# Two-layer language block with an expert stream: the second mixer's steps set further apart, its attention moved beside the recurrence, and output weight blocks loaded over 128 partitions

## The chip, the cores and the metric

The kernel runs on one core of one Trainium2 chip. The metric is the device time of one execution in microseconds. All data is float32. TensorE (PE) makes matrix products and transposes, VectorE (DVE), ScalarE (ACT) and GpSimd (POOL) compute and issue, SyncE (SP) issues the weight loads, and 16 DMA engines move the data. Each engine works through its own instructions in order and waits on semaphores for the others.

## The reference

256 tokens of width 1024 go through a first block of two layers and then through a second block of two. In the first block each layer is a mixer, an output product with a residual and a layer norm, and a sparse feed-forward layer with its own residual and norm:

```python
for i in range(2):
    z = x @ w_in                      # layer 0: mLSTM, layer 1: RG-LRU (below)
    hm = mixer(z[:, :-256]); ha = cross_attention(z[:, -256:], mem, w_kv[i])
    x = layer_norm(ALPHA * x + concat([hm, ha]) @ w_out[i])
    x = layer_norm(ALPHA * x + peer_ffn(x, w_q[i], subkeys[i], u[i], v[i]))
```

The mixer of layer 1 has 8 channel blocks of 96. Its steps are the ones that the change moves:

```python
xr = causal_conv4(z[:, 768:1536]); r = sigmoid(xr @ w_a + b_a); i = sigmoid(xr @ w_x + b_x)
a = exp(-8 * r * softplus(-lam)); u = sqrt(1 - a**2) * (i * xr)
h = scan(h * a + u)                   # over tokens
hm = h * gelu(z[:, :768])
```

Cross attention has 4 heads of 64 over 256 memory rows. The feed-forward layer takes, for each token and each of 8 heads, the 16 best of 16384 experts, and sums gelu(u_e . x) * g * v_e over its 128 experts. The second block (dilated and latent attention, gated) is not touched.

## The kernel before

The function middle() holds the part that the change touches. Its backbone is the expert stream: 2 layers x 2 token tiles of 128 tokens give 4 tiles, each with 128 slots (8 heads x 16 experts), 512 slots in all. For a slot, POOL gathers one row of u and v (8 KB) for each of the 128 tokens into one of nine row buffers (ROWS = 9, line 2712). VectorE makes the dot of the u half with x (dot, line 2225). ScalarE weighs two slots at a time (weigh, lines 2531 to 2541: gelu, gate weight, coefficient on a diagonal). TensorE adds the v half with these diagonals (line 2124). POOL issues the gather of slot n when TensorE has added slot n - 9.

All other work of the middle part stands beside the stream. Each engine runs a loop over slots and, after its work of slot n, runs those pieces of a generator beside() whose due slot, written out in `yield at + k`, is at most n. Here `at = base_of(t)` = 128 (t + 1), so the mixer of layer 1 for token tile t runs beside the stream's tile t + 1, which is the second of the four for t = 0 and the third for t = 1. Within a slot the order is: VectorE the dot, then a piece of the routing of coming slots (route, planned by plan_chunk and the loop behind it), then the mixer piece; TensorE the slot's sums, then the side piece; ScalarE, in even slots alone, the weighing of slots n and n + 1, then the side piece. An engine that waits in a side piece holds back its part of the stream.

The PSUM bank of each product is written out in `homes`, and `order` says in which order the products come, from which the semaphore counts follow. take(name) waits until the product that was in the bank before has been read; ready(name) waits for a product.

The weights pass through a ring of three slots (line 3332, on SP's queue). SP loads the block n when block n - 3 has been used. For each token tile the ring holds, in order, two blocks of w_in for xr and xq, two for the gate, three of w_out (two with 4 x 96 rows, one with 2 x 128 rows) and four of w_q (512 x 1024). SP also loads the gate matrices w_a, w_x (lines 1602, 1603) and rows of norm gains between the blocks, in its own order.

Steps of the mixer, by name and line of the kernel before: inputs, gates, memory_scores, gate_inputs (1936), turn_probabilities (1912), memory_values (1924), turn_mix (1946), out_products (1967), spread_rows (1981) and queries on TensorE; convolve (2317), the softmax maximum, the attention values (2361), the steps of the recurrence (2371 to 2400), the residual (2405) and norm on VectorE; the softmax exponentials, sigmoids (2574), decay, tanh and root (2641, 2642, 2646) and the copies out of PSUM on ScalarE.

Of the kernel before, what the change touches and what calls it, by code (L numbers as in the profile page):

```python
# [112 lines left out]
class Run:  # L113


    def __init__(self, first, count, cols, pieces, ktiles):
        self.first, self.count, self.cols, self.pieces, self.ktiles = first, count, cols, pieces, ktiles
        self.small_loads = None

# [53 lines left out]
def program(nc, a, out, parts=None):  # L173
# [1308 lines left out]
    def middle():  # L1482
# [22 lines left out]
        shared_at = place[0]  # L1505
        prob, prob_t = sb([P, XA_H, T], name="xa_prob"), sb([P, XA_H * NT, P], name="xa_probT")
        th = nc.alloc_sbuf_tensor_at("tanh_y", [RG_B, RG_G, P], F32, offset=shared_at)
        dec = nc.alloc_sbuf_tensor_at("decay", [RG_B, RG_G, P], F32, offset=shared_at + RG_G * P * 4)
# [11 lines left out]
        qT = sb([P, PE_H, 2, NT, P], name="peer_qT")  # L1520
        ids = sb([P, NT * TILE], U32, name="expert_ids")
# [116 lines left out]
        for t in range(NT):  # L1638
# [3 lines left out]
                     ("probT", t, 0): 0, ("probT", t, 1): 1, ("wa", t, 0): 0, ("wa", t, 1): 1, ("value", t): 2,  # L1642
                     ("wx", t, 0): 2, ("wx", t, 1): 0, ("haT", t): 1, ("out", t, 0): 2, ("out", t, 1): 0}
            second = {("turn", 2 * t + 3, 0): 2, ("turn", 2 * t + 3, 1): 0, ("q", t + 1, 0): 4, ("q", t + 1, 1): 1,
                      ("q", t + 1, 2): 3, ("q", t + 1, 3): 2}
            homes.update({name: places[u] for mine in (first, second) for name, u in mine.items()})
            order += spread(2 * t + 2) + list(first)
            order += spread(2 * t + 3, [places[u] for u in (3, 4, 1, 3)]) + list(second)
# [58 lines left out]
        def query_made(k, h):  # L1707
            return base_of(k - 1) + (81, 84, 92, 95)[h // 2]
# [55 lines left out]
        def tensor(pe):  # L1764
# [184 lines left out]
            def out_products(t):  # L1949
                signal, count = read_at_bank[("haT", t)]  # L1950
                pe.wait_ge(signal.sem, count)
# [45 lines left out]
            def beside():  # L1997
# [11 lines left out]
                for t in range(NT):  # L2009
# [36 lines left out]
                    yield at + 66  # L2046
                    spread_rows(2 * t + 3, slice(3, 4))
                    yield at + 70
                    turn_x(2 * t + 3)
                    yield at + 73  # L2050
                    x_read(2 * t + 3)
                    for c in range(2):
                        yield at + 74 + 11 * c
                        yield from paced(queries(t + 1, c), at + 74 + 11 * c, 6)
# [88 lines left out]
        def vector(dve):  # L2143
# [186 lines left out]
            def mixer(t):  # L2330
# [7 lines left out]
                for u, first in ((0, 29), (1, 31)):  # L2338
# [3 lines left out]
                yield at + 33  # L2342
# [5 lines left out]
                for u, first in ((2, 33), (3, 35)):  # L2348
# [6 lines left out]
                yield at + 37  # L2355
# [3 lines left out]
                yield at + 41  # L2359
# [8 lines left out]
                yield at + 43  # L2368

                dve.wait_ge(r_ready.sem, t + 1)  # L2370
                dve.tensor_tensor(r[:, :, :], r[:, :, :], sp[:, :].unsqueeze(2).to_broadcast([RG_B, RG_G, P]), ALU.mult)\
                    .then_inc(y_ready.sem, 1)
                yield at + 45

                dve.wait_ge(decayed.sem, t + 1)
                v(dve.tensor_tensor(r[:, :, :], dec[:, :, :], dec[:, :, :], ALU.mult))
                dve.scalar_tensor_tensor(out=th[:, :, :], in0=r[:, :, :], scalar=1.0, in1=th[:, :, :],
                                         op0=ALU.add, op1=ALU.mult).then_inc(square_ready.sem, 1)
                yield at + 47

                dve.wait_ge(i_ready.sem, t + 1)
                v(dve.tensor_tensor(i_g[:, :, :], i_g[:, :, :], xc[:, :, :], ALU.mult))
                yield at + 48

                dve.wait_ge(rooted.sem, t + 1)
                v(dve.tensor_tensor(i_g[:, :, :], i_g[:, :, :], th[:, :, :], ALU.mult))
                if t:
                    v(dve.tensor_tensor(last_h[:, :], last_h[:, :], dec[:, :, 0], ALU.mult))
                    v(dve.tensor_tensor(i_g[:, :, 0], i_g[:, :, 0], last_h[:, :], ALU.add))
                for g in range(RG_G):  # L2390
                    if g % 4 == 0:
                        yield at + 49 + g // 4
                    v(dve.tensor_tensor_scan(r[:, g, :], dec[:, g, :], i_g[:, g, :], 0.0, ALU.mult, ALU.add))
# [1012 lines left out]
```

## Time and profile before

| | us |
|---|---|
| median of 3 runs | 2535.95 |
| lowest, highest | 2532.78, 2541.17 |
| the profiled execution | 2532.97 |
| its span, first to last instruction | 2531.2 |
| TensorE busy | 2019.9 |
| VectorE busy | 1374.1 |
| ScalarE busy | 709.3 |
| GpSimd busy | 593.3 |

The granted TensorE clock has a mean of 0.891 of full speed over the span. The span falls into a first layer's mixer (to about 227 us), the expert stream (to about 1684 us) and the second block. In the tables below, "DMA share" is the busy share of the 16 DMA engines (sums can pass 1 by a little) and GB/s is what they moved. A row of a timeline has its start, its duration, the engine, the line, the operation, its output and inputs, and in brackets how long the engine was idle before it and for whom it waited.

### The profile page before, as it was taken

How to read it: one execution, taken by the hardware profiler on the slowest of the kernel's cores; microseconds unless marked ns; L12 is line 12 of the kernel's file. 1: busy time of each engine (PE TensorE's matmuls, PEld its weight loads, DVE VectorE, ACT ScalarE, POOL GpSimd, SP SyncE). 2: the span in 40 equal slices, each digit the busy share in tenths (PEclk: the TensorE clock that was granted, in tenths of full speed). 3: DMA queues.
4: the chain of work that ended last, by engine and by line, in shares of the span. 5: the costliest groups of instructions: out<-in, count | busy, mean ns of one | idle time of the engine just before them, and what ended most of it. 6: DMA issues, size and time to landing. Idle time of an engine off the chain costs nothing. (4 is left out here: it accounts for less than half of the span.)

```text
span 2531.2 us, 27949 instructions
## 1 busy us (share of the span) xinstructions
PE 2019.9 (80%) x10229; PEld 1055.6 (42%) x10229; DVE 1374.1 (54%) x3393; ACT 709.3 (28%) x2047; POOL 593.3 (23%) x529
## 2 busy tenths in 40 slices
PE   8998787556858866877866665669998999999998
PEld 5665344111532421442421111116875544886543
DVE  5556856768756468757568875452424422013433
ACT  1132322333343232352322433220014310014230
POOL 0002433444323444433434454420000000000000
PEclk9999899777978977887887778789999999999999
DMA  7636999999989999998999999984742242540431
GB/s 242 224 135 234 398 409 413 420 421 422 390 305 382 419 419 420 420 364 339 417 412 421 421 421 421 421 337 169 274 132 95 76 166 93 176 160 19 156 111 56
DMA packets 186820, 742.34 MB, mean 293 GB/s; under 512 B 26342, under 2 KB 45822, under 8 KB 121144
## 3 DMA queue, kind: packets, MB, share of 16 engines
q0 software_dynamic: 73728, 536.90, 52.0%
q1 hardware_dynamic: 99972, 199.72, 22.2%
q10 hardware_dynamic: 12984, 3.94, 0.7%
q8 instruction: 81, 1.33, 0.2%
q14 instruction: 55, 0.45, 0.0%
HBM read 739.39 MB, written 1.12 MB: 293 GB/s over the span
## 5 line engine op out<-in xcount | busy, mean ns | idle before, releaser
L2124 PE MATMUL psum<-expert_rows,coefs_on_diagonal 64*64 64x512 f32 x4096 | 673.5, 767 | 439.1 <-ACT coefs_on_diagonal L2541 434.5
L2712 POOL DMA_INDIRECT expert_rows<-in_peer_uv,expert_ids x512 | 588.8, 1150 | 1075.1 <-PE psum L2124 810.7
L2225 DVE SCALAR_TENSOR_TENSOR expert_rows<-expert_rows,x 128x1024 f32<-128x1024 f32 x512 | 626.5, 1225 | 375.3 <-DMA expert_rows<-in_peer_uv,expert_ids 359.8
L2124 PEld LDWEIGHTS psum<-expert_rows,coefs_on_diagonal 64*64 64x64 f32 x4096 | 145.9, 157 | 815.2 <-ACT coefs_on_diagonal L2541 610.4
L320 PE MATMUL psum<-xT,ring 128*128 128x256 f32 (+2 forms) x1472 | 322.8, 381 | 1.2 <-DMA ring<-in_mlstm_w_in 1.2
L2531 ACT ACTIVATE gelu_dots<-dots 128x2 f32<-128x2 f32 x256 | 52.1, 203 | 921.1 <-DVE expert_rows L2225 920.9
L320 PEld LDWEIGHTS psum<-xT,ring 128*128 128x128 f32 (+2 forms) x1472 | 268.8, 183 | 57.9 <-issue 10.2
L2541 ACT ACTIVATE coefs_on_diagonal<-ident,coefs 128x128 f32<-128x128 f32 x512 | 177.4, 393 | 8.3
L1800 PEld LDWEIGHTS psum<-xT,ring 128*128 128x128 f32 (+1 forms) x1088 | 130.5, 184 | 81.1 <-issue 81.1
L1800 PE MATMUL psum<-xT,ring 128*128 128x128 f32 (+1 forms) x1088 | 150.3, 289 | 0.0
L2534 ACT ACTIVATE coefs<-gelu_dots,gate_weights 128x1 f32<-128x1 f32 x512 | 123.0, 287 | 8.4
L3157 PE MATMUL psum<-ring,xT 128*128 128x512 f32 x256 | 123.5, 616 | 0.0
L2800 PE MATMUL psum<-ring,xT 128*128 128x512 f32 x192 | 86.2, 610 | 7.8 <-DVE x L2278 4.1
L1827 PEld LDWEIGHTS psum<-xT,ring 128*128 128x128 f32 x512 | 62.7, 197 | 36.8 <-issue 35.8
L1827 PE MATMUL psum<-xT,ring 128*128 128x128 f32 x512 | 71.2, 290 | 0.8 <-ACT xT L2550 0.8
L3157 PEld LDWEIGHTS psum<-ring,xT 128*128 128x128 f32 x256 | 47.5, 195 | 45.0 <-issue 43.1
L3270 ACT ACTIVATE prob<-prob,small 128x256 f32<-128x256 f32 (+3 forms) x96 | 53.2, 557 | 40.1 <-DVE small L3237 39.9
L3280 ACT COPY probT<-psum 128x256 f32<-128x256 f32 (+3 forms) x96 | 37.1, 428 | 95.5 <-PE psum L3191 95.3
L2800 PEld LDWEIGHTS psum<-ring,xT 128*128 128x128 f32 x192 | 37.3, 196 | 55.3 <-issue 51.2
L3034 PE MATMUL psum<-ring,mergedT 128*128 128x512 f32 x128 | 55.6, 594 | 2.8 <-DVEq L3307 2.8
L320 PE MATMUL psum<-ring,ymT 128*128 128x512 f32 x128 | 55.3, 592 | 0.0
L3233 DVE CUSTOM_DVE_ANT_0 prob<-psum,causal 128x256 f32<-128x256 f32 (+1 forms) x64 | 22.9, 358 | 53.6 <-PE psum L3173 52.5
(428 smaller groups left out, 2021.0 us busy)
## 6 DMA issues: line engine op xcount, KB each, us to landing
ring<-in_w_in SPq DMA_DIRECT2D x64, 1024.0 KB
ring<-in_peer_w_q SPq DMA_DIRECT2D x24, 1024.0 KB
first_modulation_weights<-in_w_ada SPq DMA_DIRECT2D x12, 1024.0 KB, 7.4
ring<-in_mlstm_w_in SPq DMA_DIRECT2D x16, 768.0 KB
ring<-in_w_ada SPq DMA_DIRECT2D x12, 1024.0 KB
expert_rows<-in_peer_uv,expert_ids POOLq DMA_INDIRECT x512
ring<-in_rglru_w_in SPq DMA_DIRECT2D x8, 1024.0 KB
ring<-in_w_out_b SPq DMA_DIRECT2D x8, 1024.0 KB
```

The source lines that it names most:

```text
L320: last = pe.matmul(o, l, r, start=first, stop=end)
L1800: ins = pe.matmul(outs[name][0:wide, c * P:(c + 1) * P], w[:, kt, col:col + wide], xT[:, i * run.ktiles + kt, t * P:(t + 1) * P], start=i ...
L1827: last = pe.matmul(out[:, b * P:(b + 1) * P], w[:, kt, b * P:(b + 1) * P], xT[:, kt, t * P:(t + 1) * P], start=kt == 0, stop=kt == KD - 1)
L2124: last = pe.matmul(psum[64 * half:64 * half + 64, 2 * t + m, :], diag[tokens, n % DIAGS, tokens], rows[tokens, at_, D + half * 512:D + (ha ...
L2225: dve.scalar_tensor_tensor(out=rows[:, at_, 0:D], in0=rows[:, at_, 0:D], scalar=1.0, in1=x[:, n // TILE % NT, :], op0=ALU.mult, op1=ALU.mu ...
L2534: ins = act.activation(coef[:, at_ + q:at_ + q + 1], gel[:, at_ + q:at_ + q + 1], ACT.Copy, scale=gw[:, g_at:g_at + 1])
L2541: ins = act.activation(diag[:, (s + q) % DIAGS, :], ident[:, :], ACT.Copy, scale=coef[:, at_ + q:at_ + q + 1])
L2712: pool_.indirect_dma_start(out=rows[:, n % ROWS, :], out_offset=None, in_=table, in_offset=bass.IndirectOffsetOnAxis(ap=ids[:, at_:at_ + 1 ...
L2800: last = pe.matmul(o, l, r, start=first, stop=end)
L3034: last = pe.matmul(o, l, r, start=first, stop=end)
L3157: ins = pe.matmul(o, l, r, start=first, stop=end)
L3270: ins = act.activation(flat, flat, ACT.Exp, bias=columns(0, step)[:, i:i + 1], accum_out=columns(1, step)[:, i:i + 1])
```

## The change

It has two parts. In the first, the due slots of the mixer's steps are moved. The convolution starts two slots later. The w_a products go from slot 40 to 39 and their sigmoids from 42 to 40; VectorE's first step on them stays in 43. Decays stay in slot 44 on ScalarE and are read in 47 instead of 45; the w_x sigmoids stay in 46 and are read in 49 instead of 47; the root comes in 48 and is read in 51 instead of 48. The attention's transposes go from 36 to 48, its values from 40 to 51, and VectorE reads them in 55 instead of 41. The output products are issued from slot 55 to 65 instead of 52 to 62, in three portions, the last one behind the wait for the turned attention output; VectorE adds them in 67 and 68 instead of 62 and 63. The norm after them, its gain rows, the turn of x and the w_q products come four to nine slots later. Bank homes and their order follow. So that the softmax's probabilities can stay until slot 48, the decays and the tanh no longer share their memory; they lie in parts of the query buffer qT that are free then.

In the second, the two w_out blocks of 4 x 96 rows are loaded with 128 partitions: each partition group k takes 128 rows from row 96 k on, so that 32 rows are loaded twice. The products still read 96 partitions.

```diff
+        dec, th = ([qT[0:RG_B, :, s, t, :] for t in range(NT)] for s in range(2))
...
+        def on_all_partitions(run, first):
+
+            run.overlapped = [(bass.AP(a["w_out"].tensor, (D + (first + k) * RG_B) * D, [[D, P], [RG_B * D, 2], [1, D]]), k)
+                              for k in (0, 2)]
+            return run
...
-            rout.append([by_rows(a["w_out"][1], 0, RG_B, 4, 0, D), by_rows(a["w_out"][1], 4 * RG_B, RG_B, 4, 0, D),
-                         by_rows(a["w_out"][1], RG_W, P, 2, 0, D)])
+            rout.append([on_all_partitions(by_rows(a["w_out"][1], i * RG_B, RG_B, 4, 0, D), i) for i in (0, 4)] + [
+                by_rows(a["w_out"][1], RG_W, P, 2, 0, D)])
...
-            return base_of(k - 1) + (81, 84, 92, 95)[h // 2]
+            return base_of(k - 1) + (85, 88, 96, 99)[h // 2]
...
 (tensor, beside)
-                    yield from paced(islice(block, 32), at + 31, 6)
-                    yield at + 36
-                    turn_probabilities(t)
-                    yield at + 37
-                    yield from paced(islice(block, 16), at + 37, 6)
-                    yield at + 40
+                    yield from paced(islice(block, 48), at + 31, 6)
+                    yield at + 39
                     gate_inputs("wa", wa, t, 0)
                     gate_inputs("wa", wa, t, 1)
-                    memory_values(t)
-                    yield at + 41
-                    yield from paced(block, at + 41, 6)
-                    yield at + 44
+                    yield at + 40
+                    yield from paced(block, at + 40, 6)
+                    yield at + 43
                     gate_inputs("wx", wx, t, 0)
                     gate_inputs("wx", wx, t, 1)
-                    yield at + 46
+                    yield at + 48
+                    turn_probabilities(t)
+                    yield at + 51
+                    memory_values(t)
+                    yield at + 55
+                    block = out_products(t)
+                    yield from paced(islice(block, 6), at + 55, 2)
+                    yield at + 58
                     turn_mix(t)
-                    yield at + 52
-                    yield from paced(out_products(t), at + 52, 2)
-                    yield at + 62
+                    yield from paced(islice(block, 10), at + 58, 2)
+                    signal, count = read_at_bank[("haT", t)]
+                    pe.wait_ge(signal.sem, count)
+                    yield at + 63
+                    yield from paced(block, at + 63, 2)
+                    yield at + 65
                     spread_rows(2 * t + 3, slice(0, 3))
...
 (vector, mixer: values after the recurrence instead of before it)
-                yield at + 45
+                yield at + 47
                 dve.wait_ge(decayed.sem, t + 1)
-                v(dve.tensor_tensor(r[:, :, :], dec[:, :, :], dec[:, :, :], ALU.mult))
+                v(dve.tensor_tensor(r[:, :, :], dec[t][:, :, :], dec[t][:, :, :], ALU.mult))
+                yield at + 48
...
-                yield at + 47
+                yield at + 49
                 dve.wait_ge(i_ready.sem, t + 1)
...
-                yield at + 48
+                yield at + 51
                 dve.wait_ge(rooted.sem, t + 1)
...
+                yield at + 55
                 out = ready(("value", t))
...
-                    yield at + 62 + half
+                    yield at + 67 + half
...
 (sync)
+                    for src, k0 in run.overlapped or ():
+                        sp.dma_start(view[:, k0:k0 + 2, :], src).then_inc(landed[slot].sem, 16)
+                    for w, row0, rows, k, k0, p0, col0 in () if run.overlapped else run.pieces:
```

## Rows read from the trace of the kernel before

**Rows 1.** The page, 40 slices of 63.3 us: GB/s of the DMA engines

```profile
GB/s 242 224 135 234 398 409 413 420 421 422 390 305 382 419 419 420 420 364 339 417 412 421 421 421 421 421 337 169 274 132 95 76 166 93 176 160 19 156 111 56
```

**Rows 2.** Windows of the stream's second, third and fourth tile of 128 slots

```profile
core 0: us, PE busy (x) PEld busy (x) DVE busy (x) ACT busy (x) POOL busy (x), PEclk, DMA share, GB/s
587.80:983.80 396.00, 287.42 (x1738) 128.32 (x1738) 257.19 (x597) 134.64 (x408) 148.82 (x128) 0.81 0.98 391
983.80:1366.60 382.80, 284.82 (x1742) 126.32 (x1742) 258.66 (x602) 136.29 (x409) 144.31 (x128) 0.83 0.99 396
1366.60:1683.80 317.20, 193.29 (x1079) 51.39 (x1078) 205.35 (x434) 108.87 (x357) 144.36 (x122) 0.81 1.00 417
```

**Rows 3.** Windows: w_out blocks loading (tile 0, tile 1), and w_q blocks loading

```profile
681.00:696.00 15.00, 11.23 (x94) 6.86 (x87) 11.63 (x30) 8.02 (x25) 4.18 (x5) 1.00 1.02 302
1081.00:1096.00 15.00, 12.16 (x88) 6.96 (x80) 11.96 (x31) 8.60 (x26) 4.83 (x4) 0.89 1.02 335
790.00:820.00 30.00, 22.89 (x102) 6.04 (x104) 17.77 (x36) 11.59 (x30) 10.58 (x10) 0.83 1.02 418
```

**Rows 4.** DMA of 675 to 725 us, then of 1070 to 1120 us

```profile
DMA packets 2757, 17.18 MB, mean 344 GB/s; under 512 B 279, under 2 KB 279, under 8 KB 1047
...
DMA packets 2829, 17.71 MB, mean 354 GB/s; under 512 B 284, under 2 KB 284, under 8 KB 1056
```

**Rows 5.** Windows in the recurrence of tile 0, of tile 1, and the emptiest 10 us

```profile
730.00:790.00 60.00, 41.08 (x165) 13.14 (x166) 42.27 (x88) 24.95 (x64) 15.12 (x15) 0.69 0.81 294
1130.00:1180.00 50.00, 34.57 (x138) 9.43 (x142) 38.19 (x87) 19.02 (x55) 13.20 (x14) 0.76 0.84 312
750.00:760.00 10.00, 3.69 (x16) 0.80 (x16) 9.52 (x22) 2.65 (x8) 2.43 (x2) 0.58 0.41 139
```

**Rows 6.** Waits of VectorE, 695 to 830 us; below the dots, one of 1095 to 1200

```profile
DVE x L2405 <- PE psum L1967: 13.0, 2, 12.8
DVE xa_out L2361 <- PE psum L1924: 7.5, 1, 7.5
DVE r L2371 <- ACT rg_e L2580: 4.7, 1, 4.7
DVE i L2382 <- ACT rg_e L2580: 4.4, 1, 4.4
DVE r L2376 <- ACT tanh_y L2642: 4.3, 1, 4.3
DVE ln_sd L2246 <- ACT ln_sd L2517: 3.1, 1, 3.1
...
DVE x L2405 <- PE psum L1967: 11.5, 1, 11.5
```

**Rows 7.** Timeline of ScalarE and VectorE around slot 43 of tile 0

```profile
721.06 0.20 ACT L2531 ACTIVATE gelu_dots<-dots 128x2 f32<-128x2 f32 x1 [10.18 <-DVE expert_rows L2225]
...
725.99 0.19 ACT L2580 COPY rg_e<-rg_e 1x1 f32<-1x1 f32 x1
...
726.28 1.22 DVE L2371 TENSOR_TENSOR r<-r,sp 96x1024 f32<-96x1024 f32 x1 [4.66 <-ACT rg_e L2580]
```

**Rows 8.** Timeline: gather and dot of the first slot, then of slot 440

```profile
226.83 1.09 POOL L2712 DMA_INDIRECT expert_rows<-in_peer_uv,expert_ids  x1 [220.53 <-DVE expert_ids L2205]
...
236.94 1.22 DVE L2225 SCALAR_TENSOR_TENSOR expert_rows<-expert_rows,x 128x1024 f32<-128x1024 f32 x1
...
1490.65 1.61 POOL L2712 DMA_INDIRECT expert_rows<-in_peer_uv,expert_ids  x1 [0.30 <-issue]
...
1507.81 1.23 DVE L2225 SCALAR_TENSOR_TENSOR expert_rows<-expert_rows,x 128x1024 f32<-128x1024 f32 x1
```

**Rows 9.** Window of slots 44 to 59 beside the mixer of tile 0

```profile
727.40:778.20 50.80, 29.28 (x117) 9.60 (x118) 40.77 (x87) 22.80 (x58) 12.78 (x12) 0.63 0.78 283
```

**Rows 10.** Timeline of TensorE beside the output products of tile 1

```profile
1157.25 1.99 PE L2124 MATMUL psum<-expert_rows,coefs_on_diagonal 64*64 64x512 f32 x8 [1.67 <-ACT coefs_on_diagonal L2541]
...
1173.79 1.09 PE L2124 MATMUL psum<-expert_rows,coefs_on_diagonal 64*64 64x512 f32 x8
1174.81 1.98 PE L1967 MATMUL psum<-ring,xr_conv 96*128 96x512 f32 x4
```

More of the change, by code:

```diff
@@ L1641, in middle @@
                      ("score", t, 0): 0, ("score", t, 1): 2, ("gate", t, 0): 3, ("gate", t, 1): 4,
[L1642 to L1645, printed above, removed]
+                     ("wa", t, 0): 0, ("wa", t, 1): 2, ("wx", t, 0): 1, ("wx", t, 1): 0,
+                     ("probT", t, 0): 2, ("probT", t, 1): 1, ("value", t): 0, ("out", t, 0): 1, ("out", t, 1): 3,
+                     ("haT", t): 2}
+            second = {("turn", 2 * t + 3, 0): 3, ("turn", 2 * t + 3, 1): 1, ("q", t + 1, 0): 0, ("q", t + 1, 1): 2,
+                      ("q", t + 1, 2): 4, ("q", t + 1, 3): 3}
             homes.update({name: places[u] for mine in (first, second) for name, u in mine.items()})
             order += spread(2 * t + 2) + list(first)
-            order += spread(2 * t + 3, [places[u] for u in (3, 4, 1, 3)]) + list(second)
+            order += spread(2 * t + 3, [places[u] for u in (4, 0, 2, 4)]) + list(second)
         last_tile = [("cols",)] + [("hT", half) for half in range(2)] + [("flip", h, part) for h in range(DA_H) for part in range(2)]
@@ L2051, in beside @@
                     x_read(2 * t + 3)
                     for c in range(2):
-                        yield at + 74 + 11 * c
-                        yield from paced(queries(t + 1, c), at + 74 + 11 * c, 6)
+                        yield at + 78 + 11 * c
+                        yield from paced(queries(t + 1, c), at + 78 + 11 * c, 6)
                 yield 3 * TILE + 2
@@ L2337, in mixer @@
                     v(dve.tensor_copy(xr[:, :, 0:CONV - 1], past[:, :, :]))
-                for u, first in ((0, 29), (1, 31)):
+                for u, first in ((0, 31), (1, 33)):
                     yield at + first
@@ L2347, in mixer @@
                 dve.tensor_scalar(negmax[:, :], rowmax[:, :], -XA_D ** -0.5, None, ALU.mult).then_inc(biased.sem, 1)
-                for u, first in ((2, 33), (3, 35)):
+                for u, first in ((2, 35), (3, 37)):
                     yield at + first
@@ L2354, in mixer @@
                     dve.tensor_copy(xr[:, 0, 0:1], xr[:, 0, 0:1]).then_inc(past_kept.sem, 1)
-                yield at + 37
+                yield at + 41
                 dve.wait_ge(exped.sem, x0 + t + 1)
                 v(dve.reciprocal(rowsum[:, :], rowsum[:, :]))
-                yield at + 41
+                yield at + 43
+                dve.wait_ge(r_ready.sem, t + 1)
+                dve.tensor_tensor(r[:, :, :], r[:, :, :], sp[:, :].unsqueeze(2).to_broadcast([RG_B, RG_G, P]), ALU.mult)\
+                    .then_inc(y_ready.sem, 1)
+                yield at + 47
+                dve.wait_ge(decayed.sem, t + 1)
+                v(dve.tensor_tensor(r[:, :, :], dec[t][:, :, :], dec[t][:, :, :], ALU.mult))
+                yield at + 48
+                dve.scalar_tensor_tensor(out=th[t][:, :, :], in0=r[:, :, :], scalar=1.0, in1=th[t][:, :, :],
+                                         op0=ALU.add, op1=ALU.mult).then_inc(square_ready.sem, 1)
+                yield at + 49
+                dve.wait_ge(i_ready.sem, t + 1)
+                v(dve.tensor_tensor(i_g[:, :, :], i_g[:, :, :], xc[:, :, :], ALU.mult))
+                yield at + 51
+                dve.wait_ge(rooted.sem, t + 1)
+                v(dve.tensor_tensor(i_g[:, :, :], i_g[:, :, :], th[t][:, :, :], ALU.mult))
+                if t:
+                    v(dve.tensor_tensor(last_h[:, :], last_h[:, :], dec[t][:, :, 0], ALU.mult))
+                    v(dve.tensor_tensor(i_g[:, :, 0], i_g[:, :, 0], last_h[:, :], ALU.add))
+                for g in range(RG_G):
+                    if g % 4 == 0:
+                        yield at + 52 + g // 4
+                    v(dve.tensor_tensor_scan(r[:, g, :], dec[t][:, g, :], i_g[:, g, :], 0.0, ALU.mult, ALU.add))
+                if t == 0:
+                    v(dve.tensor_copy(last_h[:, :], r[:, :, P - 1]))
+                yield at + 54
+                for u in range(2):
+                    signal, count = read_at_bank[("gate", t, u)]
+                    dve.wait_ge(signal.sem, count)
+                dve.tensor_tensor(xc[:, :, :], r[:, :, :], gate[:, :, :], ALU.mult).then_inc(recurred.sem, 1)
+                yield at + 55
                 out = ready(("value", t))
@@ L2409, in mixer @@
                     norm_stats(t, half)
-                yield at + 64
-                yield from norm(2 * t + 3, t, at + 62)
+                yield at + 69
+                yield from norm(2 * t + 3, t, at + 68)
             def beside():
@@ L3329, in body @@
                         sp.wait_ge(half_done[1].sem, n - (RING - 1))
-                    for w, row0, rows, k, k0, p0, col0 in run.pieces:
+                    for src, k0 in run.overlapped or ():
+                        sp.dma_start(view[:, k0:k0 + 2, :], src).then_inc(landed[slot].sem, 16)
+                    for w, row0, rows, k, k0, p0, col0 in () if run.overlapped else run.pieces:
                         src = w[row0:row0 + rows * k, :].rearrange("(k p) c -> p k c", p=rows)
```

81 lines of the change are left out of this document (26 added, 55 removed).

## The prediction

> **What bounds the kernel now.** I read the 40 slices of the page first. In the expert stream the DMA engines are full and move 420 to 422 GB/s, and two places inside it fall short, slices 12 and 13 (305, 382) and 18 and 19 (364, 339) [rows 1]; these hold the two mixers. Then I took the stream by its tiles of 128 slots [rows 2]. Without a mixer a tile takes 317.2 us, 2.48 us a slot, at 417 GB/s. With the mixer of token tile 0 it takes 396.0 us, with that of token tile 1 382.8 us. Most of that excess is bytes: 391 GB/s over 396.0 us is 154.8 MB, which at 420 GB/s would need 368.7 us. So about 27 us in the first and (151.6 MB, 360.9 us) 22 us in the second are time in which the DMA engines moved less than they can. Only that can be won, and nothing after the third tile changes. The chain of waits on the page shows the last fragments of the output layer alone and says nothing here.
>
> Windows of 10 us sort the lost time into two kinds.
>
> First, while the four blocks of w_out with 96 partitions load, the engines are busy (share 1.02) and slow: 302 GB/s, in token tile 1 335 GB/s, against 418 GB/s while w_q is loaded over 128 partitions beside the same stream [rows 3]. The 50 us around the two blocks move 17.18 MB and 17.71 MB [rows 4]; at 418 GB/s these need 41.1 and 42.4 us. Lost: 8.9 + 7.6 = 16.5 us.
>
> Second, in the recurrence the engines run dry: 294 GB/s over 60 us and 312 GB/s over 50 us, at worst a share of 0.41 [rows 5]. 17.6 MB and 15.6 MB need 42.2 and 37.3 us at 418. Lost: 17.8 + 12.7 = 30.5 us. The rest of the shortfall is in small loads, and I leave it.
>
> **Why they run dry.** VectorE waits in its mixer steps, and the dots of the stream stand behind it in order. Its waits are 7.5 us for the attention values, 4.7, 4.3 and 4.4 us for three results of ScalarE, and 13.0 us for the output products; the second tile repeats them within 1.5 us [rows 6]. One hop is plain in the timeline [rows 7]. ScalarE takes its mixer step of slot 42 only behind the weighing of the pair 42, 43, so after dot 43. VectorE asks for the result in slot 43, right after that dot. Weighing, table load, sigmoids and a copy run from 721.06 to 726.18 us, 5.1 us, and VectorE stands for 4.7 of them. The ring of nine row buffers covers only part of such stops: in the quiet tile a gather is issued 17.1 us before its dot, the first gather of all, with empty queues, needs 10.1 us [rows 8], so some 7 us are slack. VectorE's waits up to the recurrence add to 20.9 us.
>
> **Part 1: steps three slots apart.** It removes no instruction of the engines. In place of a one-slot distance VectorE now asks three slots after ScalarE's step (40 to 43, 44 to 47, 46 to 49, 48 to 51). Between ScalarE's start on the pair and the question there lie two more dots: 2 x 2.48 = 5.0 us against the 5.1 us of the hop. I take 0 to 1 us of wait per hop. The first one may keep 2 to 3 us, since TensorE's products w_a come in slot 39 behind its own queue. The attention values leave the hop altogether: softmax is done at 36, the turns come at 48, values at 51, VectorE reads at 55; 7.5 us become 0. What stands behind VectorE's new waits is as before, the dots; ScalarE's queue carries the same steps, and its new cover is the idle time that it has (busy 22.8 us of 50.8) [rows 9].
>
> VectorE's own work remains: 40.8 us in the 16 slots of the recurrence, against 16 x 2.48 = 39.7 us of rows [rows 9]. It is spread over 13 slots instead of 9, and the 7 us of slack carry it.
>
> The output products start at slot 55 instead of 52 and end at 65, VectorE reads at 67 instead of 62: two slots, 5 us, of distance where there was none. TensorE is the slow one there: 1.09 us for a slot's rows and 1.98 us for two products, 2.93 us from slot to slot [rows 10]. Ten such slots put it 10 x (2.93 - 2.48) = 4.5 us further behind. So of the 13.0 us of wait I expect 3 to 9 us to stay. It costs DMA time only beyond the slack, and from slot 59 on the first w_q block (2.1 MB, 5 us) fills the engines.
>
> Of the steps moved later: the norm waits (root 70, VectorE 73) are three slots apart too and lose their 3.1 us. The w_q products come four slots later, and the routing of the next tile with them: by the planner's arithmetic its first chunk is routed in slot 240 instead of 236, and the gather that needs it is issued after slot 247. SP's load of norm rows ahead of the last w_q block now waits for the step at 75 instead of 66, but that block's ring slot is free only at about 83. The bias tiles start five slots later, with a tile to spare. I cost these at nothing; if routing came after slot 247, each slot of it would cost 2.48 us. That decays and roots lie in the query buffer, rows 512 elements apart, is priced by no row: bound it by 0 and by a tenth of the twelve 1.1 to 1.2 us operations on them, 1.4 us a tile; I take 0.
>
> Residual: the dry time that stays is between 0 and, if the out wait and half the hops empty the ring again, 10 us a tile. I take 5 and 4 us (the first has the gate matrices' short rows too). Part 1 wins 30.5 - 9 = 21.5 us.
>
> **Part 2: the wide blocks.** Each of the four blocks becomes 512 rows of 4 KB instead of 384, 0.52 MB more, 2.1 MB in all: 5.0 us at 418 GB/s. The shape is then that of the w_q load, 128 partitions by two rows of 4 KB to a DMA, and I give it that row's rate, 418 GB/s. It wins 16.5 - 5.0 = 11.5 us. Bounds: 16.5 us less 5.0 at best; at worst the blocks stay at 302 GB/s. Then a block with its share of the stream (1 to 2) is 6.3 MB, 20.9 us, of which the stream alone would need 10.0: 10.9 us of excess against 15.5 - 7.5 = 8.0 now, so 2.9 us more per block, a loss of 11.5 us.
>
> The Trainium skill, page "SBUF — State Buffer", section on the DMA port swizzle, says that bandwidth depends on how many of 16 ports the partitions reach, and partitions 0 to 95 reach all 16. By that rule the narrow block is not slow for its width, and the wide one only adds bytes, which is what rival C works out from rows. The table in the same section of the Trainium skill puts two thirds of 96 partitions on the even ports, and 302 of 418 GB/s [rows 3] is nearer to that. The Trainium skill's section on the bandwidth-pool intuition, same page, gives HBM about 358 GB/s a core; by it the full engines lose little and only some 5 us could be won, but the trace holds 417 GB/s for 317 us [rows 2], so this gets no chance.
>
> **Sum.** Profiled execution 2533 us (span 2531.2 and 1.8 around it): 2533 - 21.5 - 11.5 = 2500 us. The median before, 2536, is 3 us higher within a spread of 8; I predict the sum's own 2500. The two gains add, as both are counted in bytes not moved in windows that do not overlap.
>
> **Rivals.**
> A, the forecast: 2500 us, own range 2492 to 2509. Chance 0.55.
> B, the out products become the bound: ring slack is spent by slot 55 and TensorE's 2.93 us a slot passes straight to the gathers. For it: the lag of 4.5 us and the wait of 13.0 us. Against: w_q fills the engines. 10 us a tile stay dry: 2511 us. Chance 0.15.
> C, the width is not what slows the block: 2533 - 21.5 + 11.5 = 2523 us. For it: no row shows a 96-partition load at full rate beside the stream, so another trait of these blocks could be the slow one. Against: the 128-partition load of the same row length has 418 [rows 3]. Chance 0.10.
> D, all of it comes back: 2533 - 30.5 - 11.5 = 2491 us. Chance 0.10.
> E, no change: C, and the waits only move to other steps (ScalarE's part won 10 us): 2534 us. Chance 0.05.
> F, slower: TensorE runs its out products at the 1.2 GHz level. The granted clock is 0.63 in the recurrence [rows 9], and at that level a slot's rows take 1.99 us [rows 10]. With products at twice 1.98 a slot is 5.95 us, ten are 59.5 us against 24.8, less 12 us of slack and w_q: 23 us a tile, 2546 us. It decides from about 8 of the 10 slots at the low level. Against: within the same stretch the row of 1173.79 has it at the full level [rows 10]. Chance 0.05.
>
> 0.3% of 2533 us, 7.6 us, is what a measurement tells from no change. Faster by more: A to D, 0.90; within: 0.05; slower: 0.05. The range 2489 to 2520 leaves out C, E and F, 0.20.
>
> **What would show it.** The third tile stays at 317 us. The tile of mixer 0 falls to about 378 us, that of mixer 1 to about 368. DMA while w_out loads is near 418 GB/s at the same share: if 300, part 2 is wrong. The three waits of VectorE for ScalarE are under 1 us each and that for the values is gone: if 4 us stand there still, part 1 is wrong. The out wait is 3 to 9 us. No 10 us in the recurrence has a DMA share under 0.8. The prediction falls if VectorE waits for expert ids' routing, or the out products show the low clock.

## The result, and the profile after

The changed kernel takes 2505.1 us (median of 4 runs, 2503.8 to 2507.9), the kernel before 2538.6 us in the same comparison (2532.8 to 2543.4). The ratio is 0.9871, 95% interval 0.985 to 0.9892: 33.5 us faster by the medians. The two profiled executions stand 29.2 us apart (2532.97 and 2503.82 us, spans 2531.2 and 2502.0 us). The forecast was 2500 us, range 2489 to 2520.

The tiles of the stream after the change, windows as in [rows 2] (length, busy time and count of each engine, granted clock, DMA share, GB/s):

```profile
587.00:967.00 380.00, 283.89 (x1730) 125.61 (x1730) 253.01 (x581) 138.40 (x410) 148.95 (x128) 0.82 1.02 414
967.00:1336.40 369.40, 278.00 (x1738) 124.31 (x1738) 259.39 (x601) 137.44 (x410) 147.76 (x128) 0.84 1.01 411
1336.40:1653.60 317.20, 196.43 (x1083) 52.77 (x1083) 209.56 (x449) 109.65 (x359) 143.03 (x121) 0.79 1.00 415
```

The tile with the mixer of token tile 0 fell from 396.0 to 380.0 us and the next from 382.8 to 369.4 us. The third window was cut to the length of the one before, so its 317.2 us say nothing; from the first to the last dot the quiet tile takes 320.3 us instead of 319.4. All of the gain is in the two tiles that were forecast to give it. The DMA engines now move 414 and 411 GB/s there instead of 391 and 396.

While the w_out blocks load, the same two windows as in [rows 3], then the 50 us around the blocks of token tile 0 as in [rows 4]:

```profile
681.00:696.00 15.00, 12.81 (x90) 7.75 (x87) 12.95 (x34) 11.26 (x30) 5.01 (x5) 0.89 1.02 417
1081.00:1096.00 15.00, 13.45 (x112) 8.59 (x109) 7.10 (x13) 11.52 (x28) 6.35 (x6) 1.00 1.02 417
...
DMA packets 3497, 20.85 MB, mean 417 GB/s; under 512 B 318, under 2 KB 318, under 8 KB 1592
```

The share is the same 1.02 as before, the rate 417 instead of 302 and 335 GB/s, and 50 us carry 20.85 MB instead of 17.18. The same engines, as busy, move a fifth more.

VectorE's waits, two stretches that answer to [rows 6], token tile 0 and then 1 (us in total, times, longest):

```profile
DVE expert_rows L2234 <- DMA expert_rows<-in_peer_uv,expert_ids: 55.4, 35, 2.7
DVE x L2415 <- PE psum L1971: 2.2, 2, 1.9
...
DVE expert_rows L2234 <- DMA expert_rows<-in_peer_uv,expert_ids: 30.9, 17, 3.2
DVE expert_rows L2234 <- issue: 2.4, 1, 2.4
DVE x L2415 <- PE psum L1971: 2.1, 1, 2.1
DVE r L2371 <- ACT rg_e L2590: 0.5, 1, 0.5
```

The three waits for ScalarE (but for 0.5 us in token tile 1), the one for the attention values and the one for the norm's root are gone, that for the output products is 2 us. What VectorE waits for now is rows, as it should in a stream that the DMA engines bound. The same hop as in [rows 7], timeline of both engines:

```profile
702.94 0.20 ACT L2541 ACTIVATE gelu_dots<-dots 128x2 f32<-128x2 f32 x1 [6.08 <-DVE expert_rows L2234]
...
707.88 0.19 ACT L2590 COPY rg_e<-rg_e 1x1 f32<-1x1 f32 x1
...
709.36 1.23 DVE L2234 SCALAR_TENSOR_TENSOR expert_rows<-expert_rows,x 128x1024 f32<-128x1024 f32 x1 [1.69 <-DMA expert_rows<-in_peer_uv,expert_ids]
...
711.23 1.22 DVE L2371 TENSOR_TENSOR r<-r,sp 96x1024 f32<-96x1024 f32 x1
```

ScalarE needs the same 5.1 us (702.94 to 708.07). VectorE asks at 711.23, 3.2 us after the result is there, and does not wait for it; it has spent the hop on two dots and on waits for rows.

Slots 44 to 56 and then 56 to 68 of token tile 0, then the same of token tile 1, and the emptiest 10 us, windows:

```profile
712.40:750.10 37.70, 23.64 (x144) 9.54 (x136) 33.91 (x77) 22.76 (x52) 14.65 (x12) 0.72 1.01 415
750.10:782.40 32.30, 31.93 (x128) 9.75 (x129) 19.31 (x37) 12.22 (x39) 11.03 (x11) 0.90 1.04 371
...
1091.20:1130.70 39.50, 22.38 (x144) 9.48 (x144) 31.97 (x77) 27.30 (x61) 15.46 (x12) 0.76 1.00 406
1130.70:1162.10 31.40, 31.26 (x128) 9.52 (x129) 24.52 (x53) 8.62 (x32) 13.43 (x11) 0.93 0.92 360
...
1130.00:1140.00 10.00, 9.16 (x36) 2.77 (x40) 9.62 (x27) 3.16 (x13) 4.16 (x3) 0.73 0.79 287
```

The recurrence is no longer dry. What is still lost lies behind it: 32.3 us at 371 GB/s and 31.4 us at 360 GB/s are, against 418, 3.6 and 4.4 us (length x (1 - rate / 418)); with 0.3 and 1.1 us of slots 44 to 56 that makes 9.4 us.

### The profile page after: what moved, and what is told of

The parts are those of the page before. It is cut to its first block and busy times, and to the rows that moved or that the text cites. A ratio compares the mean times of both kernels' runs of the same rounds, so it can differ in the third digit from the quotient of the medians.

```text
span 2502.0 us, 27950 instructions
## 1 busy us (share of the span) xinstructions
PE 2011.0 (80%) x10229; PEld 1049.1 (42%) x10229; DVE 1375.0 (55%) x3393; ACT 715.0 (29%) x2051; POOL 604.8 (24%) x529
## 5 line engine op out<-in xcount | busy, mean ns | idle before, releaser
L2722 POOL DMA_INDIRECT expert_rows<-in_peer_uv,expert_ids x512 | 600.2, 1172 | 1034.5 <-PE psum L2133 771.9
```

The costliest lines, as they stand in the source:

```text
L2722: pool_.indirect_dma_start(out=rows[:, n % ROWS, :], out_offset=None, in_=table, in_offset=bass.IndirectOffsetOnAxis(ap=ids[:, at_:at_ + 1 ...
```

## The experiments

Every run was timed beside the kernel before on its own chip. The last column is the time from the first to the last dot of the stream. It leaves out the stretches before and behind the stream, which no experiment changes, but it is read from one execution of each kernel.

| kernel | median us | ratio to before, 95% interval | stream us |
|---|---|---|---|
| before | 2537 to 2539 | | 1449.0 |
| changed | 2505.1 | 0.9871, 0.985 to 0.9892 | 1420.2 |
| e1, steps only | 2514.9 | 0.9907, 0.9884 to 0.993 | 1430.9 |
| e2, wide blocks only | 2522.2 | 0.9932, 0.991 to 0.9954 | 1440.0 |
| e3, three hops of one slot | 2512.7 | 0.9894, 0.987 to 0.9919 | 1426.5 |
| e4, values read in 52 | 2502.4 | 0.9852, 0.983 to 0.9875 | 1420.5 |
| e5, 112 partitions | 2518.9 | 0.9918, 0.99 to 0.9936 | 1435.4 |
| e6, 64 and 32 partitions | 2522.6 | 0.9935, 0.9917 to 0.9952 | 1437.6 |
| e7, output products paced | 2501.5 | 0.9854, 0.9836 to 0.9872 | 1418.3 |
| e8, matrices loaded once | 2497.0 | 0.9836, 0.9815 to 0.9856 | 1415.5 |
| e9, e7 and e8 together | 2497.6 | 0.9841, 0.9821 to 0.9861 | 1413.5 |
| e10, one hop of one slot | 2502.6 | 0.9859, 0.9835 to 0.9883 | 1419.7 |
| e11, attention back in front | 2504.5 | 0.9869, 0.9848 to 0.989 | 1420.6 |
| e12, sums read in 65 | 2502.5 | 0.9855, 0.9838 to 0.9872 | 1420.6 |

The medians of kernels whose streams agree within 1 us (changed, e4, e10, e11, e12) lie between 2502.4 and 2505.1, so a difference of 3 us between medians means nothing here. The first and the last tile of the stream, in which nothing differs between these experiments, take 349.5 to 351.5 us and 319.1 to 320.4 us, so a difference of 1 to 2 us in the last column means little too.

**The two parts alone.** e1 is the changed kernel with the narrow blocks:

```diff
-            rout.append([on_all_partitions(by_rows(a["w_out"][1], i * RG_B, RG_B, 4, 0, D), i) for i in (0, 4)] + [
-                by_rows(a["w_out"][1], RG_W, P, 2, 0, D)])
+            rout.append([by_rows(a["w_out"][1], 0, RG_B, 4, 0, D), by_rows(a["w_out"][1], 4 * RG_B, RG_B, 4, 0, D),
+                         by_rows(a["w_out"][1], RG_W, P, 2, 0, D)])
```

> The changed kernel with the two w_out blocks loaded over 96 partitions again. Theory (the narrow blocks slow every packet beside them): 302 to 335 GB/s at a DMA share of 1.02 while they load, 3 us more per block, 11.5 us in all: about 2516 us (2513 to 2520). Rival (the change's gain is the steps alone, the width costs or gives nothing; only 2.1 MB fewer are loaded): 2500 us.

2514.9 us, and the stream is 10.7 us longer. The rate beside the narrow block in e1, window:

```profile
681.00:696.00 15.00, 12.09 (x87) 7.61 (x84) 10.11 (x27) 10.30 (x26) 4.51 (x4) 0.89 1.02 327
```

The rival is out: the width costs what was worked out. e2 is the reverse, the kernel before with the wide blocks (the diff's second part alone).

> The kernel before with the two w_out blocks loaded over 128 partitions, steps as they were. Theory (the two gains add): 2538 less 11.5: about 2527 us, the recurrence runs dry as before (about 17 and 12 us of DMA time lost). Rival (gathers that land earlier before the recurrence only wait there, since VectorE sets the pace): under 4 us gained, 2535 us or more.

2522.2 us, 14.9 us faster by the medians, 9.0 us by the stream. Slots 28 to 44 and 44 to 56 of token tile 0, then of token tile 1, windows of e2:

```profile
662.20:722.70 60.50, 49.15 (x368) 29.95 (x368) 40.52 (x102) 23.91 (x72) 18.45 (x17) 0.94 1.02 417
722.70:766.00 43.30, 21.17 (x105) 7.29 (x102) 33.38 (x75) 20.03 (x48) 11.45 (x10) 0.68 0.78 289
...
1049.20:1109.50 60.30, 48.97 (x376) 30.56 (x376) 38.95 (x89) 26.58 (x74) 19.10 (x18) 0.97 1.02 418
1109.50:1154.80 45.30, 23.82 (x94) 7.88 (x94) 34.95 (x87) 20.82 (x50) 10.49 (x10) 0.62 0.80 304
```

The blocks load at full rate and the recurrence behind them runs dry as before. In token tile 0 the gain arrives: that tile of the stream takes 386.6 us instead of 396.1. In token tile 1 it does not: 383.3 against 382.7 us. There the rival holds: rows that land sooner only wait, since VectorE's stops come next. In one profile each the parts give 18.1 and 9.0 us alone and 28.8 us together: in sum they add to within 1.7 us. By tile they do not. In token tile 1 the wide blocks give nothing alone and 5.9 us once the stops are gone (375.3 us in e1, 369.4 changed); in token tile 0 they give 9.5 us alone and 5.2 us then (385.2 and 380.0).

**Which stops cost.** e3 sets three of VectorE's steps back to one slot behind ScalarE's; e10 sets back the decays alone (the second and third pair of lines):

```diff
-                yield at + 43
+                yield at + 41
                 dve.wait_ge(r_ready.sem, t + 1)
...
-                yield at + 47
+                yield at + 45
                 dve.wait_ge(decayed.sem, t + 1)
...
-                yield at + 48
+                yield at + 46
                 dve.scalar_tensor_tensor(out=th[t][:, :, :], in0=r[:, :, :], scalar=1.0, in1=th[t][:, :, :],
...
-                yield at + 49
+                yield at + 47
                 dve.wait_ge(i_ready.sem, t + 1)
```

> The changed kernel with the three steps of VectorE that read ScalarE's results (sigmoids of w_a, decays, sigmoids of w_x) back to one slot after ScalarE's step: 41, 45 and 47 instead of 43, 47 and 49; the attention stays where it is. Theory: VectorE waits 4.3 to 4.7 us at each again, 13.4 us a token tile. By the two traces 20.9 us of waits before stood for 13.4 us more dry DMA time, 0.64 us each, so 8.6 us a tile: about 2522 us (2515 to 2530). Rival (the ring of nine buffers covers these waits, the attention's move made the gain): 2505 to 2509 us.

2512.7 us, stream 6.3 us longer. Both sides missed: the waits came (below), but they cost under half of what 0.64 us for each us of wait would give. In token tile 1 the same three waits were 7.4, 7.2 and 4.7 us. Waits of VectorE in e3, token tile 0:

```profile
DVE r L2371 <- ACT rg_e L2590: 4.5, 1, 4.5
DVE i L2383 <- ACT rg_e L2590: 4.4, 1, 4.4
DVE r L2376 <- ACT peer_qT L2646: 4.3, 1, 4.3
```

> The changed kernel with one step alone, the decays, read by VectorE one slot after ScalarE's step (45 instead of 47, the square in 46). VectorE waits some 4.3 us in each token tile. If a wait reaches the end in proportion (three of them cost 8 us in all), 2 to 3 us: 2507 to 2508 us and 1 to 2 us of DMA time lost in slots 44 to 56 of a tile. If the nine buffers cover the first 6 to 7 us of waits and no more: 2505 us, under 1 us more lost.

2502.6 us, stream 0.5 us shorter: the wait of 4.3 us (4.8 in token tile 1) costs nothing at the end. Slots 44 to 56 of both token tiles in e10, windows:

```profile
712.60:752.30 39.70, 22.56 (x144) 9.44 (x136) 33.84 (x76) 22.57 (x52) 13.64 (x12) 0.79 1.00 398
...
1090.80:1131.00 40.20, 22.81 (x144) 9.47 (x144) 31.89 (x78) 26.72 (x59) 15.34 (x12) 0.71 0.98 387
```

In these slots 1.9 and 3.0 us of DMA time are lost, 3.5 us more than in the changed kernel, and yet the two tiles of the stream take 378.8 and 370.0 us against 380.0 and 369.4. DMA time lost in a window of a dozen slots is not yet time lost at the end.

e4 moves VectorE's read of the attention values from `at + 55` to `at + 52`, in front of the scans.

> The changed kernel with VectorE reading the attention values in slot 52, one slot after TensorE's step, instead of 55. Theory: VectorE waits some 7 us for the product in each token tile, 4.5 us of it reach the end: about 2514 us (2508 to 2520). Rival (a single wait is covered by the ring): within 2 us of 2505.

2502.4 us, stream the same. But the wait was 1.3 and 1.6 us and not 7, so e4 tells nothing about a wait of 7 us; I had taken the size over from a place where TensorE does other products in the same slot. e11 puts it right. It starts from e2, keeps the attention in its old place and sets the rest apart (ScalarE's sigmoids of w_a stay in slot 42; its decays, sigmoids of w_x and root go to 46, 48 and 50):

```diff
-                yield at + 43
+                yield at + 45
                 dve.wait_ge(r_ready.sem, t + 1)
...
-                yield at + 45
+                yield at + 49
                 dve.wait_ge(decayed.sem, t + 1)
...
-                yield at + 47
+                yield at + 51
                 dve.wait_ge(i_ready.sem, t + 1)
...
-                yield at + 48
+                yield at + 53
                 dve.wait_ge(rooted.sem, t + 1)
...
-                    yield from paced(out_products(t), at + 52, 2)
+                    yield from paced(out_products(t), at + 57, 2)
...
-                    yield at + 62 + half
+                    yield at + 69 + half
```

> The steps set three slots apart (and all behind them later), but the attention where it was before: transposes in 36, values in 40, read by VectorE in 41, in front of the recurrence; blocks of 128 partitions as in the changed kernel. VectorE waits 6 to 9 us for the values again and 0 to 1 us at each of the three hops. If the nine buffers cover one wait of that size and no more: 1 to 3 us over the changed kernel, 2506 to 2508 us. If the attention's move made most of part 1 (three hops alone gave only 8 of its some 20 us): 2513 us or more.

2504.5 us, stream within 0.4 us of the changed kernel. VectorE's waits in e11, token tile 0 and then 1; then windows, slots 44 to 56 of token tile 0, and slots 28 to 44 and 44 to 56 of token tile 1:

```profile
DVE xa_out L2368 <- PE psum L1931: 5.8, 1, 5.8
DVE r L2378 <- ACT rg_e L2588: 0.5, 1, 0.5
...
DVE xa_out L2368 <- PE psum L1931: 8.0, 1, 8.0
...
DVE r L2378 <- ACT rg_e L2588: 2.8, 1, 2.8
```

```profile
712.40:749.00 36.60, 21.72 (x142) 8.21 (x146) 33.45 (x75) 27.79 (x64) 14.70 (x12) 0.82 1.01 420
...
1037.40:1093.30 55.90, 46.56 (x346) 29.20 (x344) 43.32 (x106) 17.64 (x54) 17.67 (x17) 0.94 1.01 412
1093.30:1130.70 37.40, 21.06 (x138) 7.87 (x142) 29.62 (x70) 31.64 (x72) 14.78 (x12) 0.83 1.00 405
```

A stop of 5.8 and one of 8.0 us stand just in front of slot 44 (behind the second one more of 2.8 us, where 0 to 1 was expected), and the engines stay full or nearly so: slots 28 to 68 of token tile 1 lose 7.1 us of DMA time, against 5.6 us in the changed kernel. With the distances in place, the move of the attention gives nothing. Without them it does: e3 has the move and the short distances, and its stream is 13.6 us shorter than that of e2, which has neither (nor the distance of the output products and the norm). So neither the move nor the distances alone made the gain of part 1; each takes stops out of a row. Put in order of waits in a row per token tile: none (changed) 0 us over both tiles; one of 4.3 to 4.8 us (e10) 0; one of 5.8 and one of 8.0 us (e11) 0; three, 13.2 us in token tile 0 and 19.3 in token tile 1 (e3), 6 to 8 us; four, 19.4 and 22.3 us (e2), 17 to 20 us, of which some may belong to e2's waits for the output products, 14.4 and 12.8 us. The nine row buffers cover a stop of about 8 us, and not three that follow each other within a few slots. Which tile pays is not shown: in e3 the tile times rise by 0.8 and 5.7 us, the DMA time lost in slots 44 to 68 by 7.2 and 2.9 us.

e12 has VectorE add the output products in `at + 65 + half` instead of `at + 67 + half`.

> The changed kernel with VectorE adding the output products in 65 and 66 instead of 67 and 68. VectorE waits some 7 us there instead of 2. If that distance matters: 3 to 6 us more over the two token tiles, 2509 us. If VectorE only runs ahead of TensorE there and the w_q blocks keep the DMA engines full behind it: 2505 to 2506 us.

2502.5 us, stream within 0.4 us, with waits of 7.2 and 9.8 us. The two slots of distance gave nothing. Slots 56 to 68 of the two token tiles take 36.1 and 36.4 us instead of 32.3 and 31.4, at 377 and 366 GB/s, so the DMA engines go on at the rate they had. That w_q blocks fill them there is the likely reason; no run takes these away.

**The width.** e5 loads 112 partitions, e6 the 96 rows of each group once, by two DMAs of 64 and of 32 partitions:

```diff
-            run.overlapped = [(bass.AP(a["w_out"].tensor, (D + (first + k) * RG_B) * D, [[D, P], [RG_B * D, 2], [1, D]]), k)
+            run.overlapped = [(bass.AP(a["w_out"].tensor, (D + (first + k) * RG_B) * D, [[D, 112], [RG_B * D, 2], [1, D]]), k)
...
-                        sp.dma_start(view[:, k0:k0 + 2, :], src).then_inc(landed[slot].sem, 16)
+                        sp.dma_start(view[0:112, k0:k0 + 2, :], src).then_inc(landed[slot].sem, 16)
```

> The changed kernel with 112 partitions instead of 128 in the two w_out blocks (448 rows, 1.84 MB a block). Theory 1 (only the full 128, 8 to each of 16 engines as in the stream's own loads, runs at full rate; 6 or 7 to an engine do not): 300 to 340 GB/s as with 96, 2515 to 2519 us. Theory 2 (the halves of the partitions are loaded unevenly, 64 to 48 instead of 64 to 32): about 366 GB/s, 2508 us. Theory 3 (96 is odd, 112 is not): 418 GB/s, 2503 to 2504 us.

```diff
+            run.overlapped = [(bass.AP(a["w_out"].tensor, (D + first * RG_B + p) * D, [[D, n], [RG_B * D, 4], [1, D]]), (p, n))
+                              for p, n in ((0, 64), (64, 32))]
...
+                    for src, (p, n) in run.overlapped or ():
+                        sp.dma_start(view[p:p + n, 0:4, :], src).then_inc(landed[slot].sem, 16)
```

> The changed kernel with each w_out block of 4 x 96 rows (no row twice) loaded by two DMAs, one of partitions 0 to 63 and one of 64 to 95, both over all four row groups, instead of two DMAs over 128 partitions. If the uneven halves are what slows (theory 2), it stays slow, 300 to 340 GB/s: 2513 to 2517 us. If it is the number of partitions that falls to an engine (6), 4 and 2 to an engine may run freely at 418 GB/s and save the 2.1 MB: 2500 us.

The window of 681 to 696 us in e5, then in e6:

```profile
681.00:696.00 15.00, 9.31 (x76) 5.97 (x72) 10.67 (x27) 5.93 (x16) 3.96 (x4) 0.99 1.03 312
```

```profile
681.00:696.00 15.00, 9.85 (x71) 5.25 (x70) 8.92 (x22) 8.27 (x22) 2.81 (x3) 0.91 1.02 292
```

Both are slow at a full share. e5 differs from the changed kernel in the width alone (the narrow blocks too were loaded by two DMAs of two rows per partition each). Its 112 partitions give 312 GB/s, no more than 96, so it is not the share of the halves (366 GB/s expected of that), and it carries more bytes: 2518.9 us, worse than the 2514.9 us of the narrow block. 64 and 32 are the worst, 2522.6 us, over both figures of the expectation; their DMAs have four rows per partition, so here the width is not the only difference. Of the widths tried only 128 is fast, and why is not shown.

**What is left.** e7 spreads the output products, one a slot from 55 and two a slot from 61, and what stands behind them comes two to four slots later.

```diff
-                    yield from paced(islice(block, 6), at + 55, 2)
-                    yield at + 58
+                    yield from paced(islice(block, 6), at + 55, 1)
+                    yield at + 61
                     turn_mix(t)
-                    yield from paced(islice(block, 10), at + 58, 2)
+                    yield from paced(islice(block, 10), at + 61, 2)
```

> The changed kernel with the first 6 output products one to a slot (55 to 60) and the other 14 two to a slot (61 to 67) instead of all 20 two to a slot from 55; VectorE adds them in 70 and 71, and the norm, the turn and the w_q products come three slots later. In the changed kernel nearly all DMA time still lost lies in slots 56 to 68 (3.7 and 4.4 us). Theory (TensorE's 2.93 us a slot passes to the gathers, 10 x 0.45 = 4.5 us a tile): with 2.0 us a slot in six of them under 1 us stays lost, 2505 less 6 to 8: about 2498 us. Rival (VectorE, 96% busy in the 10 us before, empties the ring and TensorE only follows): 2503 to 2506 us.

2501.5 us, between the two figures, and the stream is 1.9 us shorter. But 1.0 and 0.7 us of that are in the stream's first and last tile, which the edit does not touch; the tiles beside the mixers take 379.8 and 369.4 us against 380.0 and 369.4. Slots 56 to 68 of token tile 0 in e7 and then of token tile 1, windows:

```profile
751.60:782.90 31.30, 29.37 (x127) 8.04 (x128) 17.82 (x34) 12.05 (x38) 12.44 (x12) 0.91 1.03 370
...
1132.10:1159.20 27.10, 26.18 (x117) 7.22 (x118) 23.65 (x56) 8.80 (x32) 13.83 (x11) 0.92 0.95 379
```

In token tile 0 370 GB/s against 371 without the edit: taking away TensorE's pace alone changes nothing there. In token tile 1 slots 44 to 68 lose 2.6 instead of 5.5 us, though the tile is no shorter. In token tile 0 the share over 1 at that rate pointed to the load that falls into it, the gate matrices for token tile 1. e8 loads them once; r and i go to the part of qT that the other token tile uses.

```diff
-        wa_at = place[0]
-        r = sb([RG_B, RG_G, P], name="r")
-        wa = nc.alloc_sbuf_tensor_at("w_a", [RG_B, RG_G, RG_B], F32, offset=wa_at)
...
+        wa, wx = sb([RG_B, RG_G, RG_B], name="w_a"), sb([RG_B, RG_G, RG_B], name="w_x")
...
+        rs, i_gs = ([qT[0:RG_B, :, s, 1 - t, :] for t in range(NT)] for s in range(2))
...
-        rq[1][0].small_loads = lambda sp: gate_matrices(sp, 1)
```

> The changed kernel with the gate matrices w_a and w_x loaded once, not again for token tile 1 (they no longer share memory with r and i, which move into the half of the query buffer that the other token tile uses). Theory (the time lost in slots 56 to 68 of token tile 0, 3.7 us, is this load: 0.59 MB in rows of 384 B, 321 GB/s at a DMA share of 1.06; its bytes alone are 1.4 us more): 3 to 4 us faster, 2501 to 2502 us, under 1.5 us lost there. Rival (TensorE's output products are what is lost there, in both token tiles): 1.4 us faster for the bytes, 2503 to 2504 us, 3 us or more still lost.

2497.0 us, stream 4.7 us shorter: more than either figure. The tile with mixer 0 in e8, and its slots 56 to 68, windows:

```profile
587.00:961.90 374.90, 281.80 (x1730) 126.03 (x1730) 252.87 (x581) 138.23 (x410) 146.56 (x128) 0.83 1.01 416
```

```profile
750.50:782.50 32.00, 31.66 (x128) 9.61 (x129) 19.19 (x36) 12.19 (x38) 11.77 (x11) 0.91 0.99 385
```

That tile goes from 380.0 to 374.9 us. 1.4 us of the 5.1 are bytes (0.59 MB at 418 GB/s). The other 3.7 us go with the load too, but only 1.1 of them are found in the slots where it runs (3.6 us lost there before, 2.5 now); that all of them are the slowness of its short rows is not shown, as e8 also moves r and i. 2.5 us stay lost in that window, at 385 GB/s, where under 1.5 were expected. e9 has both edits.

> The paced output products and the gate matrices loaded once, together. If the loss in token tile 0 is the matrices and that in token tile 1 the output products (paced alone lost 3.6 in tile 0 as before and 2.5 instead of 5.5 us in tile 1), the two add: 2505 less 3 less 4, about 2498 us, the fastest so far. If either hides the other: 2501 us.

Slots 56 to 68 of token tile 0 in e9, window:

```profile
752.60:780.70 28.10, 27.75 (x126) 7.55 (x126) 17.78 (x35) 12.09 (x39) 12.21 (x11) 0.94 1.00 409
```

409 GB/s, 0.6 us lost. So that window was held down by both, the matrices and TensorE's pace, and the pace shows only once the matrices are gone (371 to 370 GB/s with them, 385 to 409 without). 2497.6 us, about the 2498 expected, though e8 alone had reached it; stream 2.0 us under e8, 1.1 of them in the two tiles beside the mixers. By the medians e8 and e9 are the same, and e8 is the smaller edit. Both are faster than the changed kernel as far as these runs can tell: the intervals of the ratios overlap (0.9815 to 0.9856 and 0.9821 to 0.9861 against 0.985 to 0.9892), but the streams are 4.7 and 6.7 us shorter, and all ten executions, up to 2500.65 us, lie below the fastest of e10 on the same chip, 2500.84 us, whose stream is that of the changed kernel.

## Why the prediction was right

- **What bounds the kernel.** Right: DMA bytes in the full stretches, and lost DMA time in two places. Counting bytes not moved and pricing them at 418 GB/s gave 33 us; the stream gave 28.8, the profiled executions 29.2 and the medians 33.5. That the medians meet the forecast so closely is partly luck: the median before lies 5.6 us above its profiled execution, the median after 1.3 us. The mechanism was right and the size some 4 us high, 3.4 of them in part 1.
- **The length of a slot.** The 317.2 us of the quiet tile run from its first dot to its 127th, which is 126 slots and not 128: a slot takes 2.51 us, not 2.48. It changes little. Two dots still cover 5.0 us, the output products' lag is 4.2 us instead of 4.5, and VectorE's 40.8 us in 16 slots stand against 40.2.
- **The wide blocks, 11.5 us.** Right: 417 GB/s after, e1 gives 10.7 us by the stream and 9.8 by the medians. Rival C is out.
- **Part 1, 21.5 us.** 18.1 us by the stream in e1, 22.3 by its medians. The residual of 5 and 4 us came out as 3.9 and 5.5 (slots 44 to 68). Its reasons came out in part. In token tile 0 the load of the gate matrices, which the prediction had only named in passing, was the larger part: without it the tile is 5.1 us shorter (e8). The pace of TensorE, which it had made the main one, gave 0.2 us in the two tiles when it alone was taken away (e7) and 1.1 us once the matrices were gone (e9). What holds token tile 1 back behind slot 56 stays open in part. Rival B, 10 us a tile, is out.
- **The hops.** Right in mechanism: 5.1 us of ScalarE behind two dots, waits of 0 to 0.5 us. I had kept 2 to 3 us for the first; 0.5 at most came. The 7 us of slack were read from a single gather, 17.1 us ahead of its dot (the median of slots 400 to 479 is 15.6), but stops of 5.8 and 8.0 us did cost under 1 us (e11).
- **The attention.** The wait of 7.5 us went, as said. That its end is worth something beside the distances was wrong (e11); it is worth something only while other stops stand behind it (e3 against e2). The prediction added up 20.9 us of waits; the runs showed that one of up to 8.0 us costs nothing, and three of 13.2 us or more in a row do.
- **The output products.** I expected 3 to 9 us of wait to stay; 2 us stayed, and e12 shows that 7 to 10 us there would cost nothing either.
- **Steps at nothing.** VectorE's operations on the strided operands took 1222 to 1245 ns, before 1220 to 1222, and no wait for expert ids arose between the tiles. Rival F did not occur: the output products ran at 1.98 us for two in all but the first slot (3.16 us in token tile 0, 2.42 in 1).
- **The signs.** The tiles of 380.0 and 369.4 us (378 and 368 forecast), the 417 GB/s and the short waits for ScalarE came as said. One sign was missed by little: 10 us with a DMA share of 0.79 (1130 to 1140 us), where token tile 1's recurrence ends and the output products begin; none under 0.8 was expected.

## What to carry to other kernels

Where an engine serves a stream in order and also asks another engine for results, count the distance in slots of the stream. Here 5.1 us of hop over 2.5 us of slot, and one slot more because ScalarE handles them in pairs, gave three; one and three slots were run, two was not. A buffer ring covers one stop of about its slack, so look for stops that follow each other and part those, and leave single ones alone. When DMA is the bound, compare GB/s at equal busy share: here a load over fewer partitions slowed the whole stream beside it, and a wider one with useless bytes was cheaper.

## What the runs showed of the hardware

- A load of rows of 4 KB over 96, 112 or 64 and 32 partitions beside a 128-partition gather brought the sum of both to 302 to 335, 312 and 292 GB/s at a DMA share of 1.02 or 1.03; over 128 partitions the sum was 417. The share alone would not have shown it. Why is open. The Trainium skill, page "DMA: Bandwidth & Descriptors", section on the descriptor swizzle, says that in a 128-partition transfer each engine writes to one port alone. No run here looked at ports. It is a guess, and no more, that 96, 112, 64 and 32 partitions, dealt evenly to 16 engines as 6, 7, 4 and 2, do not keep an engine to one port.
- Without one load of 0.59 MB in rows of 384 B the stream was 4.7 us shorter (e8); its bytes alone are 1.4 us at 418 GB/s. The 10 us from 750 us on ran at 321 GB/s and a share of 1.06 with it, at 380 GB/s and 0.97 without.
- VectorE and ScalarE took the same time, to within 2%, on operands whose rows lie 2 KB apart (8 rows of 128 elements) as on one contiguous run: for 96x1024, VectorE 1222 to 1245 ns (before 1220 to 1222), ScalarE 1056 ns for the decays (before 1057).
